# Decay exponents of a state-space layer: from matrix products on TensorE to a round trip through DRAM and a subtraction on GpSimd

## The reference

```python
a_cs = jnp.cumsum(d * a, axis=2)                       # running sum over the chunk, one per head
seg = a_cs[:, :, :, None] - a_cs[:, :, None, :]        # l x s differences
decay = jnp.exp(jnp.where(causal, seg, -jnp.inf))
cb = jnp.einsum('bclgn,bcsgn->bclsg', cc, bc)
y_diag = jnp.einsum('bclsgr,bcsgrp->bclgrp', cb[..., None] * decay, xdt)
```

## Time and profile before

| what | value |
|---|---|
| median of 3 runs | 2773.87 us |
| the runs | 2773.5, 2773.87, 2775.04 us |
| span of the profiled execution, first to last instruction | 2771.6 us |
| TensorE busy | 2748.3 us, 99% |
| VectorE, ScalarE, GpSimd busy | 1604.5, 1183.0, 1096.0 us |
| granted clock of TensorE | 0.999 of full speed |
| moved by DMA | 505.65 MB, mean 182 GB/s |

### The profile page before, as it was taken

One profiled execution on the slowest core, in us unless ns is written; L12 is line 12 of the kernel. 1 busy time (PEld: TensorE's weight loads), 2 busy tenths in 40 slices (PEclk: granted clock), 3 DMA queues, 4 the chain that ended last, 5 costly groups with the idle time before them and its releaser, 6 DMA issues.

```text
span 2771.6 us, 35692 instructions
## 1 busy us (share of the span) xinstructions
PE 2748.3 (99%) x13342; PEld 2298.7 (83%) x13342; DVE 1604.5 (58%) x2236; ACT 1183.0 (43%) x2110; POOL 1096.0 (40%) x799
## 2 busy tenths in 40 slices
PE   8999999999999999999999999999999999999998
PEld 6788888888888888888888888888888888888887
DVE  4687623666426665147673466664444666666666
ACT  2465544455325554155542545554454332222223
POOL 1365541223101222002233578866555435353434
PEclk9999999999999999999999999999999999999999
DMA  9765486443456335554436456584344942333323
GB/s 293 242 216 193 159 295 236 183 169 136 183 197 228 122 122 190 188 207 176 150 121 241 163 178 243 197 300 164 134 162 146 361 157 92 124 134 123 128 92 152
DMA packets 215786, 505.65 MB, mean 182 GB/s; under 512 B 12970, under 2 KB 96558, under 8 KB 206142
## 3 DMA queue, kind: packets, MB, share of 16 engines
q1 hardware_dynamic: 215614, 503.37, 50.4%
HBM read 357.57 MB, written 145.75 MB: 182 GB/s over the span
## 4 chain that ended last, share of the span: by engine, by line
PE 97%; DVE 1%; issue 1%; DMA 1%; POOL 0%; ACT 0%; DVEq 0%; POOLq 0%; ACTq 0%
PE bank L2024 22%; PE bank L1692 21%; PE bank L1992 21%; PE bank L1736 13%; PE bank L1716 7%; PE bank L1827 3%; PE bank L1832 2%; PE bank L1811 1%; PE bank L1633 1%; PE bank L1794 1%; PE bank L1783 1%; PE bank L1817 1%; PE bank L1805 1%; PE bank L1755 1%; PE bank L1947 0%
## 5 line engine op out<-in xcount | busy, mean ns | idle before, releaser
L1692 PE MATMUL bank<-hnT_hi,w_ring 128*128 128x512 f32 x1152 | 374.7, 396 | 0.0
L2161 DVE SCALAR_TENSOR_TENSOR acc<-pre,par,acc 128x512 f32<-128x512 f32 x240 | 217.1, 904 | 108.0 <-ACT pre L1230 102.3
L2024 PE MATMUL bank<-w_first,T_hi 128*128 128x512 f32 x896 | 275.9, 389 | 0.9 <-issue 0.9
L1692 PEld LDWEIGHTS bank<-hnT_hi,w_ring 128*128 128x128 f32 x1152 | 216.4, 188 | 44.9 <-ACT win_tmp L1339 0.5
L1992 PE MATMUL bank<-T_hi,w_both 128*128 128x512 f32 x768 | 242.1, 389 | 0.2 <-DVE ff L2444 0.2
L1736 PE MATMUL bank<-w_ring,T_hi 128*128 128x512 f32 x768 | 241.9, 396 | 0.0
L2503 DVE TENSOR_TENSOR acc_th<-bank,acc_th 128x512 f32<-128x512 f32 x224 | 149.9, 686 | 153.9 <-PE bank L2024 153.7
L983 POOL TENSOR_TENSOR small<-small 128x1 f32<-128x1 f32 (+1 forms) x71 | 17.9, 252 | 528.8 <-ACT yo L1313 322.3
L1692 PE MATMUL bank<-hnT_lo,w_ring 128*128 128x512 f32 x576 | 224.4, 390 | 0.0
L2024 PEld LDWEIGHTS bank<-w_first,T_hi 128*128 128x128 f32 x896 | 168.1, 188 | 36.0 <-issue 1.2
L1716 PE MATMUL bank<-w_ring,hnT_hi 128*128 128x384 f32 x768 | 197.9, 338 | 0.0
(11 more groups left out here) (310 smaller groups left out, 6339.7 us busy)
## 6 DMA issues: line engine op xcount, KB each, us to landing
w_ring<-w_scr SPq DMA_DIRECT2D x312, 512.0 KB, 4.2
T_scr<-stage SPq DMA_DIRECT2D x32, 1792.0 KB, 6.5
w_scr<-w_both SPq DMA_DIRECT2D x104, 512.0 KB, 4.0
pair_raw<-in_w_ff SPq DMA_DIRECT2D x36, 1024.0 KB, 5.4
third<-T_scr SPq DMA_DIRECT2D x28, 1024.0 KB, 4.8
pair_raw<-T_scr SPq DMA_DIRECT2D x28, 1024.0 KB, 4.8
raw<-in_w_in SPq DMA_DIRECT2D x36, 512.0 KB, 5.5
w_raw<-in_w_ff SPq DMA_DIRECT2D x12, 1024.0 KB, 7.4
```

Of the source, the lines that this page charges most:

```text
L1692: mm = nc.tensor.matmul(bank[s][:, :], w[:, k, :], t[:, k, :], start=(k == 0 and j == 0), stop=(k == KT - 1 and j == 2))
L2024: mm = nc.tensor.matmul(bank[4 * half + t][:, :], a[:, k, tok], w[:, k, :], start=(SECOND[q % 7] not in GOES_ON and k == 0 and j == 0), st ...
L2161: ins = nc.vector.scalar_tensor_tensor(acc[:, s, 0:TB], pre[:, s, k:k + TB], w, acc[:, s, 0:TB], ALU.mult, ALU.add)
```

## The change

The exponents aren't made on TensorE any more. After the running sums of a block are transposed into PSUM, ScalarE copies them to `acsT` in one piece (24 rows, one for each head). SyncE stores the rows to a DRAM tensor `sums_scr` in four transfers, waits for them, and loads the sums of the four chunks of group 0 back, each with every partition reading the same 768 numbers (`load_sums`). The loads of the groups after it are issued when the Exp of the same chunk in the group before is done. GpSimd subtracts the running sum of the partition's own token, six heads at a time, in place (`difference`), one step ahead of its use. ScalarE makes Relu and Exp from SBUF in all blocks, and VectorE masks `cb` with `tri` in all blocks. `seg_l`, `seg_s`, `running_sums`, `negated_sums`, the selectors and the mask products are gone.

```diff
@@ sync @@
+                def store_sums(b):
+                    acsT_ready.wait(sp, b, 1)
+                    for g in range(GROUPS):
+                        rows = slice(g * HEADS_PER_GROUP, (g + 1) * HEADS_PER_GROUP)
+                        sp.dma_start(sums_scr[b, g].rearrange("c (r l) -> r c l", l=P),
+                                     acsT[rows, :].rearrange("r (c l) -> r c l", l=P)
+                                     ).then_inc(sums_stored.sem, 16)
+                def load_sums(b, g, c):
+                    if g:
+                        exp_ready.wait(sp, b, (g - 1) * CH + c + 1)
+                    sp.dma_start(sums[:, c, :, :].rearrange("p r l -> p (r l)"),
+                                 sums_scr[b, g, c].partition_broadcast(P)
+                                 ).then_inc(sums_loaded[c].sem, 16)
...
                         load(N0 + n, in_unit(n))
+                        if n == 11:
+                            store_sums(b)
+                            sums_stored.wait(sp, b, 16 * GROUPS)
+                            for c in range(CH):
+                                load_sums(b, 0, c)
+                        g, j = divmod(n, UNITS_G)
+                        if g >= 2 or g == 1 and j >= 5:
+                            after = {5: 0, 7: 1, (0 if b else 1): 2, 3: 3}.get(j)
+                            done = g if j >= 5 else g - 1
+                            if after is not None and 0 < done < GROUPS:
+                                load_sums(b, done, after)
@@ gpsimd @@
+                def difference(b, q):
+                    g, c = divmod(q, CH)
+                    sums_loaded[c].wait(pool, b, 16 * (g + 1))
+                    acs_ready.wait(pool, b, 1)
+                    o = c * HEADS + g * HEADS_PER_GROUP
+                    nc.gpsimd.tensor_tensor(
+                        sums[:, c, :, :], sums[:, c, :, :],
+                        acs[:, o:o + HEADS_PER_GROUP].unsqueeze(2).to_broadcast(
+                            [P, HEADS_PER_GROUP, P]), ALU.subtract
+                        ).then_inc(difference_ready.sem, 1)
...
                     for q, g, c, n1, n2 in mixer_plan(b):
+                        if q == 0:
+                            difference(b, 0)
                         if b == 0 and n1 is not None:
                             low_part(pool, N0 + n1 + 2)
...
+                        if q + 1 < STEPS:
+                            difference(b, q + 1)
@@ scalar @@
-                        ab_ps.wait(act, b, q + 1)
+                        difference_ready.wait(act, b, q + 1)
                         ydiag_ps.wait(act, b, q)
...
+                        nc.scalar.activation(E[:, :, :], sums[:, c, :, :], ACT.Relu, scale=-1.0
+                                             ).then_inc(fall_ready.sem, 1)
+                        fall_ready.wait(act, b, q + 1)
+                        nc.scalar.activation(E[:, :, :], E[:, :, :], ACT.Exp, scale=-1.0
+                                             ).then_inc(exp_ready.sem, 1)
@@ tensor, slot1 @@
-                    if b == 0:
-                        for j in range(2):
-                            nc.tensor.matmul(
-                                bank[4 + j][:, 0:GW].rearrange("p (r l) -> p r l", l=P),
-                                ident_r[:, :], barred[:, :].unsqueeze(1).to_broadcast([P, 3, P]),
-                                start=True, stop=False)
-                    for j in range(2):
-                        mm = nc.tensor.matmul(
-                            bank[4 + j][:, 0:GW].rearrange("p (r l) -> p r l", l=P),
-                            seg_s[:, g % 2, cols], seg_l[:, c, 3 * j:3 * j + 3, :],
-                            start=b > 0, stop=True)
-                    mm.then_inc(ab_ps.sem, 1)
@@ vector @@
-                        if b:
-                            steps.link(nc.vector.tensor_tensor(cb, cb, tri[:, :], ALU.mult))
+                        steps.link(nc.vector.tensor_tensor(cb, cb, tri[:, :], ALU.mult))
```

109 lines of the change are left out of this document (18 added, 91 removed).

## The result

The changed kernel is slower. Four runs took 2803.36 to 2808.98 us, median 2805.4, against 2773.68 for four runs of the kernel before on the same chip: ratio 1.0116, 95% interval 1.0101 to 1.0130. That is 32 us more; the forecast was 2770.6, and neither the range to 2790 nor the far end of rival B, 2794, reaches it.

A forecast was written before the change was run, and what follows sets the result against it. TensorE, busy for 2748.3 of 2771.6 us, was taken to bound the kernel. The terms -31.9 + 9.6 + 11 + 4 + 4 = -3.3 us gave 2770.6 us, with 8 in 10 between 2755 and 2790.

The forecast's parts named there:

- rival B: SyncE's blocked queue at each mixer's start makes weights late: slower, 2784 as middle, 2794 at the far end; chance 0.20.
- last groups: Last group of each block, one unit a step: 0.2 to 0.3 us a step, 16 steps, 4 us, bounds 0 and 12.
- starts of blocks 1 to 3: TensorE waits at slot3(0) for the new chain, 3.2 us a block: 9.6 us, bounds 3 and 24.
- a new wait of TensorE costs its length: Whole kernel: any new wait of TensorE costs its full length.
- Saving, -31.9: Exponent and mask products leave TensorE: 48 steps x 0.41 + 16 x 0.76 = 31.9 us, bounds 28.7 and 35.1.
- Start of block 0, 11: Weight splits wait behind SyncE's stalled queue, delaying TensorE: 11 us in all, bounds 5 and 20.
- unit 10: Block 0's start: its high and low parts come late behind unit 8's store; TensorE loses 5.9 us.
- Unit 11, priced at 1.9: Block 0's start: split at 148.5, wanted by TensorE at 146.6, 1.9 us more lost.
- I count that as just in time: First z units of blocks 1 to 3: weights in at 537, TensorE wants them at 536.
- The steps, "0.3 us a step over 12 steps": Block 0: Relu and tri mask lengthen each step; 0.3 us over 12 steps, 4 us, bounds 0 and 14.
- A: Round trips at the mixers' starts are hidden: faster, 2753 us; chance 0.26.
- C: VectorE and GpSimd hold each other in block 0's steps and the last groups: slower, 2787 us; chance 0.12.

The follow-up runs named there:

- run 2: The changed kernel without the store of the sums and SyncE's wait; loads read the same amount from rows of x instead: 2781.68 us, ratio 1.0029.
- pause run: The kernel before with nine TensorE pauses behind the step's first unit, each a chain of 11 tiny GpSimd products: 2793.3 us, ratio 1.0067.
- run 10: The changed kernel with GpSimd's subtraction on one head in six, 128 columns in place of 768: 2796.52 us, ratio 1.0079.
- run 4: The changed kernel with sums of blocks 1 to 3 made one item earlier, their store, wait and loads ahead of z weights: 2800.2 us, ratio 1.0093.
- run 5: The changed kernel, block 0 only: sums stored and loaded after unit 12, not 11, and low_part(10) ahead of the first subtraction: 2798.24 us, ratio 1.0088.
- kernel of 2769.98 us: The rearranged kernel (2780.4 us) with x loaded later, early subtraction in every block's last group, yo before the pool tile in block 0's last step: ratio 0.9986.

## Why the prediction was wrong

The saving was right to 3.3 us. The losses were forecast at 9.6 + 11 + 4 + 4 = 28.6 us and came to 60.4. Three steps failed: the last groups (forecast 4 us, measured 13.1 + 7.1), the starts of blocks 1 to 3 (9.6, measured 23.2), and the sentence under both, that a new wait of TensorE costs its length, with no term for the clock behind it (some 18 us by the estimate above).

- **Saving, -31.9.** Measured -28.6, at the lower bound: the follower stands 0.70 us behind the state product, not 0.65.
- **Start of block 0, 11.** The first steps were right (store behind the wait, high part at 135.17 against 134.5 forecast, 6.93 us at unit 10 against 5.9, of which 0.2 is that TensorE was free at 131.86 and not at 132.07). Unit 11, priced at 1.9, had no wait. It came to 15.1: the waits up to step 2 are 6.93, 2.42 (for VectorE's state sum) and 1.33 us (for T_lo), together 10.7, and TensorE works 8.7 us at 0.50 in the first two slow stretches, half of which is 4.4.
- **Start of blocks 1 to 3, 9.6 in all.** The waits at slot3(0) were 1.84, 2.13 and 2.54 us, less than the 3.2 I priced. The loss was 23.2, near the upper bound of 24; without the round trip 9.2 of it stayed (run 2). Two things failed. "I count that as just in time" for the z units: in blocks 2 and 3 they waited 2.35 and 2.27 us. And I priced a wait at its length alone: TensorE works 17.1 us at 0.50 at these three starts, 8.5 us lost by the estimate, and a wait of 1.84 us cost 3.7 in the pause run.
- **The steps, "0.3 us a step over 12 steps", and the last groups, "0.2 to 0.3 us a step".** The second is the term of the sum that failed worst: 4 us, bounds 0 and 12, and 20.2 measured. The first was too high. Steps 2 to 11 of block 0 lost 1.5 us in all. Its last group lost 13.1: I worked out the last group from block 1's rows, where GpSimd has nothing but the mixer, and spread block 0's loss evenly over its first twelve steps. In block 0's last group `low_part` stands on GpSimd ahead of the sums and the subtraction, and a step has one unit to hide it. Moving the subtraction took 6.9 us off there. Another 3.38 us wait there is for yo, behind a collision of VectorE with `low_part` (last section). The last groups of blocks 1 to 3 lost 2.4 us each in place of 1, and 0.9 with a subtraction of one head.
- **Rivals.** A is out. B named the mechanism of the largest part, SyncE's blocked queue: 23.7 us go with the round trip (run 2). But it put 20 us on block 0's next units, where 15.1 were lost, and 8 on all the steps and last groups, where 22.1 were. C was priced too high as a cause: steps 2 to 11 of block 0, where it should have cost 1 us a step, lost 1.5 us in all, and run 10 takes 8.9 us off with the subtraction at 0.64 in place of 1.71 us. Its mechanism is real, as the last section shows.

The runs' gains overlap and don't add up to a split of the 32 us by cause: 23.7 without the round trip, 6.3 by the earlier subtraction, 8.9 by a short one are 38.9. The 25 MB more of traffic had no run of its own.

## What to carry over

A round trip through DRAM isn't priced by its latency, but by what stands in its queue ahead of it and what it keeps back behind it: issue the store as soon as the data exist, load only the first piece at once, and let nothing big share the queue. On a kernel whose TensorE is always busy, price each new wait of 5 us or more at its length plus about 2.5 us, and put a range of 0 to 3.4 us on top of waits of about 2 us. Work the last group of a stage out by itself, from its own rows: block 0's lost 13.1 us, its other twelve steps 16.6.

## What the runs showed of the hardware

The slow clock behind a wait doesn't grow with the wait: 2.7 us more for waits of about 5 us, 2.4 for waits of about 8.

For waits of about 2 us the clock isn't to be told from the length. Behind 1.84 us in block 1 of the changed kernel it stood at 0.50 for 6.8 us of work, behind 1.84 us in the third pause run for 3.4 us. Behind 2.54 us in block 3 of the changed kernel (`slot3(0)`, 1275.2 us) it stayed at 1.00 for the next 8 us. The wait of 2.15 us for T_lo in block 0's last group is in the changed kernel and in runs 2, 4, 5 and others; the clock fell behind it in the changed kernel and in run 4, not in runs 2 and 5. The waits of 1.12 to 1.14 us in the pause run never brought it down.

VectorE and GpSimd exclude each other in SBUF, but a VectorE instruction that reads one of its two inputs from PSUM isn't held. GpSimd's `low_part` and VectorE's instructions beside it, in the kernel of 2769.98 us (start, us, engine):

```profile
175.97 2.40 POOL L502 TENSOR_TENSOR w_both<-raw,w_both 128x1024 fp32r<-128x1024 f32 x1 [0.81 <-ACT w_both L494]
...
348.04 2.37 POOL L502 TENSOR_TENSOR w_both<-raw,w_both 128x1024 fp32r<-128x1024 f32 x1 [1.42 <-ACT w_both L494]
```

```profile
176.07 0.56 DVE L2225 TENSOR_TENSOR y<-bank,ty 128x384 f32<-128x384 f32 x1 [3.99 <-PE bank L1833]
176.66 2.12 DVE L2227 TENSOR_TENSOR y<-y,zs 128x384 f32<-128x384 f32 x1
...
348.11 2.33 DVE L2185 COPY phist<-pre 128x16 f32<-128x16 f32 x1
```

The sum of `bank` (in PSUM) and ty has 384 columns and starts 0.10 us behind `low_part`. It takes 0.56 us, as everywhere (0.54 to 0.56 us in all 64), beside a running `low_part`. The product of y and zs, of the same shape and with both inputs in SBUF, starts 0.59 us later and takes 2.12 in place of 0.56: it ends 0.41 us behind `low_part`. This is the instruction whose mean of 1583 ns the forecast quoted. A copy of 16 columns that took 0.17 elsewhere takes 2.33. It goes the other way round too: where y with zs starts first (222.41 us, 0.56 us long), the `low_part` that starts 0.02 us behind it takes 2.80 us. The Trainium skill, page "SBUF — State Buffer", section "Who interferes with whom", has it that the ports which the two engines share are an exclusive lock, that whoever issues first has them for the whole instruction, and that the other blocks fully; the trace agrees, with 1.6 and 2.2 us added, about the rest of `low_part`'s length. In the changed kernel's last step of block 0 such a collision makes VectorE's sum of a pool tile 2.82 us long, 2.1 more than its 0.71 elsewhere, and these 2.1 us are most of TensorE's wait of 3.38 us for yo, which VectorE makes behind it:

```profile
361.50 2.35 POOL L502 TENSOR_TENSOR w_both<-raw,w_both 128x1024 fp32r<-128x1024 f32 x1 [0.65 <-ACT w_both L494]
...
361.59 2.82 DVE L2188 TENSOR_TENSOR acc<-pre 128x527 f32<-128x527 f32 x1
...
366.38 1.01 PE L1828 MATMUL bank<-xw,xb 128*128 128x384 f32 x1 [3.38 <-DVE yo L2319]
```
